# A decoder step on one core: where the index-key page copies, the bias scratch write and the input loads stand in their queues

## What is computed

```python
def swiglu(h, w_gate, w_up, w_down):
    return (jax.nn.silu(h @ w_gate) * (h @ w_up)) @ w_down

for i in range(DEPTH):                       # DEPTH = 2, D_FF = 2688
    xp = xp + 0.5 * swiglu(rmsnorm(xp, ffn_norm[i, 0]), ...)
    xs = xs + 0.5 * swiglu(rmsnorm(xs, ffn_norm[i, 0]), ...)
    # i = 0, mixer A: an indexer scores all keys, top-k of them are attended
    ki_all = concatenate([cache_idx[layer, page_table].reshape(b, past, IDX_DIM), ki], axis=1)
    # i = 1, mixer B: sliding window with sinks
    # both add rel_bias(dist, table), 32 log buckets x 16 heads
    xp = xp + 0.5 * swiglu(rmsnorm(xp, ffn_norm[i, 1]), ...)
y = rmsnorm(x, final_norm)
```

## Time and profile before

| what | us |
|---|---|
| median of 3 runs | 2751.65 (2748.27 to 2754.09) |
| span of the profiled execution, first to last instruction | 2739.2 |
| median of the runs less that span | 12.45 |
| TensorE matmuls busy | 2444.2 (89% of the span) |
| GpSimd busy | 1040.7 (38%) |
| VectorE busy | 1134.8 (41%) |
| DMA | 195.6 MB, mean 71 GB/s |

### The profile page before, as it was taken

How to read it: one execution, slowest core, us unless ns; L and a number is a source line. 1 busy time by engine, 2 the same in 40 slices (tenths; PEclk the granted TensorE clock), 3 DMA queues, 4 the chain that set the end, 5 groups by cost and what they waited for, 6 DMA issues and landing times.

```text
span 2739.2 us, 42110 instructions
## 1 busy us (share of the span) xinstructions
PE 2444.2 (89%) x16399; PEld 2236.9 (82%) x16399; DVE 1134.8 (41%) x1299; ACT 370.8 (14%) x778; POOL 1040.7 (38%) x620
## 2 busy tenths in 40 slices
PE   4999998999467676889999999999988888999997
PEld 3999998539345444889999999999986678999997
DVE  3444322147999322454443244442214435444312
ACT  2000000220123211010000010000012321000001
POOL 2556554204000000245555545555541004555552
PEclk9999999759567777999999999999996569999998
DMA  7433433503001223123333333333351002333331
GB/s 137 95 90 89 106 84 76 102 0 95 0 1 31 62 76 101 39 62 84 84 82 82 89 77 77 83 81 81 83 129 39 1 8 63 83 84 81 80 80 55
DMA packets 377742, 195.60 MB, mean 71 GB/s; under 512 B 66323, under 2 KB 374380, under 8 KB 377644
## 3 DMA queue, kind: packets, MB, share of 16 engines
q1 hardware_dynamic: 365216, 178.61, 26.4%
q10 hardware_dynamic: 12220, 15.73, 2.4%
q0 software_dynamic: 224, 0.16, 0.0%
HBM read 188.17 MB, written 11.62 MB: 73 GB/s over the span
## 4 chain that ended last, share of the span: by engine, by line
PE 81%; DVE 11%; SPq 4%; issue 2%; ACT 1%; DMA 1%; POOL 0%; DVEq 0%; ACTq 0%; POOLq 0%
PE psum L472 69%; PE psum L589 2%; DVE scsA L1445 1%; DVE mx8A L1443 1%; SPq L350 1%; SPq L385 1%; PE psum L564 1%; PE psum L659 1%; SPq L357 1%; PE psum L757 1%; PE psum L748 1%; DVE scpA L1445 1%; PE psum L579 1%; DVE mx8pA L1443 1%; PE psum L626 1%
## 5 line engine op out<-in xcount | busy, mean ns | idle before, releaser
L472 PE MATMUL psum<-XH,WSP 128*128 128x288 f32 (+1 forms) x6688 | 1171.9, 297 | 28.2 <-POOL WSP L434 13.0
L472 PEld LDWEIGHTS psum<-XH,WSP 128*128 128x128 f32 (+1 forms) x6688 | 991.5, 190 | 33.7 <-issue 13.8
L432 POOL CAST WSP<-WST 128x1024 fp32r<-128x1024 f32 (+1 forms) x305 | 310.0, 1016 | 1619.2 <-PE psum L472 1477.1
L434 POOL TENSOR_TENSOR WSP<-WST,WSP 128x1024 fp32r<-128x1024 f32 (+1 forms) x305 | 730.0, 2394 | 24.4
L472 PE MATMUL psum<-XL,WSP 128*128 128x288 f32 x3344 | 719.5, 297 | 0.0
L472 PEld LDWEIGHTS psum<-XL,WSP 128*128 128x128 f32 x3344 | 542.6, 190 | 0.0
L472 PE MATMUL psum<-GH,WSP 128*128 128x288 f32 x2688 | 465.7, 295 | 0.0
L472 PEld LDWEIGHTS psum<-GH,WSP 128*128 128x128 f32 x2688 | 394.1, 188 | 0.0
L472 PE MATMUL psum<-GL,WSP 128*128 128x288 f32 x1344 | 286.7, 295 | 0.0
L1177 DVE TENSOR_TENSOR us<-psum,rstd 128x576 f32<-128x576 f32 x84 | 63.7, 758 | 478.4 <-PE psum L472 478.4
L1150 DVE SCALAR_TENSOR_TENSOR X<-psum,X 128x576 f32<-128x576 f32 x48 | 36.4, 758 | 438.9 <-PE psum L472 438.9
(11 more groups left out here) (213 smaller groups left out, 1678.3 us busy)
## 6 DMA issues: line engine op xcount, KB each, us to landing
WST<-in_ffn_w_gate SPq DMA_DIRECT2D x168, 256.0 KB, 3.8
WST<-in_ffn_w_up SPq DMA_DIRECT2D x168, 256.0 KB, 3.9
WST<-in_ffn_w_down SPq DMA_DIRECT2D x192, 224.0 KB, 3.6
WST<-in_a_w_in SPq DMA_DIRECT2D x28, 256.0 KB, 4.6
kv0A<-in_cache_kv SPq DMA_DIRECT2D x48, 128.0 KB, 2.3
kv1A<-in_cache_kv SPq DMA_DIRECT2D x48, 128.0 KB, 2.3
WST<-in_b_w_in SPq DMA_DIRECT2D x20, 256.0 KB, 3.8
kscr<-in_cache_idx SPq DMA_DIRECT2D x128, 32.0 KB, 2.0
```

What stands on the lines that cost most here:

```text
L432: nc.gpsimd.tensor_copy(WSP[s][:, 0, 0:width], WST[s][:, 0:width]).then_inc(w_hi, 1)
L434: nc.gpsimd.tensor_tensor(WSP[s][:, 1, 0:width], WST[s][:, 0:width], WSP[s][:, 0, 0:width].bitcast(F32), ALU.subtract).then_inc(w_split, 1)
L472: ins = mm(out[0:width, h, :], w[:, part, b * width:(b + 1) * width], x[:, h * HALF:(h + 1) * HALF], start=first and k == 0, stop=last and ...
```

## The change

Three edits.

- In ffn0's gate loop the sync engine issues the six weight loads of a pass first, then the page copies of request i. The copies of request 7 stay behind the loop.
- ScalarE issues the identity, then x, then the other five constants.
- The DMA that writes gscr moves from ahead of update(0) to behind ffn0's gate loop on ScalarE, ahead of update(1), and the wait for it to behind update(1). gvec gets space of its own beside GH and GL.

```diff
@@ memory @@
             us = sb(c, "us", [P, TOK])
+            gvec = sb(c, "gvec", [HEADS, GW])
...
-            gvec = sb(c, "gvec", [HEADS, GW])
@@ sync engine, ffn @@
                 with sp.Fori(0, NF // RING) as i:
+                    for j in range(2 * RING):
+                        chunk(n0 + j, i, 2 * RING, cols((wg, wu)[j % 2], (i * RING + j // 2) * P))
                     if name == "ffn0":
                         gather_keys(i)
-                    for j in range(2 * RING):
-                        chunk(n0 + j, i, 2 * RING, cols((wg, wu)[j % 2], (i * RING + j // 2) * P))
                 if name == "ffn0":
                     for b in range(NF // RING, NB):
                         gather_keys(b)
@@ ScalarE @@
+            act.dma_start(ident[:, :], io["c_ident"]).then_inc(const_in, 16)
+            for t in range(NTT):
+                src = ...
+                act.dma_start(xtok[0:src.shape[0], t, :], src).then_inc(x_in, 16)
-            for dst, src in ((ident[:, :], io["c_ident"]), (grows[0:4 * ND, :], ...
+            for dst, src in ((grows[0:4 * ND, :], ...
                 act.dma_start(dst, src).then_inc(const_in, 16)
-            for t in range(NTT):
-                src = ...
-                act.dma_start(xtok[0:src.shape[0], t, :], src).then_inc(x_in, 16)
...
+            act.wait_ge(gain_set, 1)
+            update(0)
+            ffn("ffn0")
             act.wait_ge(g_set, 1)
             act.dma_start(bass.AP(tensor=gscr, ...), gvec...).then_inc(g_out, 16)
-            act.wait_ge(gain_set, 1)
-            update(0)
+            update(1)
             act.wait_ge(g_out, 16)
-            ffn("ffn0")
-            update(1)
```

More of the change, by code:

```diff
@@ L1000, in window_sample_attention @@
                        bank[(7, 3)[half]][0:NT, :], ACT.Copy).then_inc(ms["ptnS_evac"], 1)
-            for dst, src in ((ident[:, :], io["c_ident"]), (grows[0:4 * ND, :], io["ffn_norm"].rearrange(
+            act.dma_start(ident[:, :], io["c_ident"]).then_inc(const_in, 16)
+            for t in range(NTT):
+                src = io["x_prompt"][0, t * P:(t + 1) * P, :] if t < NQT else \
+                    io["x_sample"].rearrange("b t d -> (b t) d")
+                act.dma_start(xtok[0:src.shape[0], t, :], src).then_inc(x_in, 16)
+            for dst, src in ((grows[0:4 * ND, :], io["ffn_norm"].rearrange(
                     "l s (d p) -> (l s d) p", p=P)), (grows[4 * ND:6 * ND, :], io["mix_norm"].rearrange(
@@ L1006, in _ @@
                 act.dma_start(dst, src).then_inc(const_in, 16)
-            for t in range(NTT):
-                src = io["x_prompt"][0, t * P:(t + 1) * P, :] if t < NQT else \
-                    io["x_sample"].rearrange("b t d -> (b t) d")
-                act.dma_start(xtok[0:src.shape[0], t, :], src).then_inc(x_in, 16)
             act.wait_ge(gain_ps, 1)
```

## The result

The changed kernel runs in 2780.05 us (median of 4 runs, 2768.36 to 2784.07), the kernel before in 2750.28 (4 runs beside them): a ratio of 1.0097, 95% interval 1.0075 to 1.012. The forecast was 2781.7 (2759 to 2791), slower. The profiled execution has a span of 2778.3 us. Of all runs in this document two were slow ones, 3125.86 and 3873.18 us, both of the kernel with the write moved alone; they are in its median and not in its ratio.

A forecast was written before the change was run, and what follows sets the result against it. The prediction took TensorE, holding 81% of the chain, to bound the kernel. Start -10.6, stall +38.8 and restart +1.8 sum to +30.0 us, added to the median 2751.65: 2781.7 us, range 2759 to 2791.

The forecast's parts named there:

- step 1: Start of ffn0, loads before gathers and x moved forward: first projection at 43.7 instead of 54.27, gain 10.6 us.
- Between the passes: Gate loop of ffn0: one batch still stands between two groups of six loads, so nothing changes.
- step 2: End of the gate loop: two batches instead of one before the first down load, a stall of 16.8 us from order alone.
- step 3: End of the gate loop: batch 7's gathers meet the scratch write, making the whole stall 38.8 us (16.8 to 42.4).
- The reckoning beside the row: Batch 7 beside the write: packet turns of 2.1 to 4.0 us, the batch ending near 357 even at 2.1.
- Rival B: End of the gate loop: gathers pass at 0.79 us, the first down load meets the write; +8 to +19 us, chance 0.17.
- step 4: TensorE after the new stall: matmuls run slowly until the clock recovers, costing 1.8 us.
- The frame: Whole kernel: the median is 12.4 us over the profiled span, and the change is added to the median.

The follow-up runs named there:

- x alone: The changed kernel with the sync engine waiting for x before its first weight load: 2780.79 us, ratio 1.0112.
- The doubling: The changed kernel with a second scratch write of the same size behind the first, to a scratch nobody reads: 2812.77 us, ratio 1.0219.
- the four with pieces: Changed kernel with batch 7 in the first pass and the write cut into 8 DMAs: 2741.48 us; three variants with further start edits: 2740.57, 2756.58, 2737.37.

## Why the prediction was right

The mechanism and the place hold. The size holds in part by luck: the terms found sum to +34.2 us and those forecast to +30.0. The start was put 3.1 too good and the stall 1.4 too low, which add up, and only 0.3 of the restart goes the other way. That the medians are 29.8 apart, so close to 30.0, owes something to the matmuls' pace and to mixer A, of which the forecast had nothing.

**The start, step 1: right in kind, 3.1 us too high.** The gain was put at 10.6 (range 5.6 to 15.1) and is 7.5. The mis-sized term is the landing of x and the constants beside three weight loads: 12.7 was reckoned from the two rates, and the constants' matmul begins at 15.60. Two errors stand in that term. The reckoning took 3 x 256 KB for the three chunks, while a chunk is two DMAs of 256 KB; the list of DMA issues of the changed kernel's first 16 us has six:

```profile
WST<-in_ffn_w_gate SPq DMA_DIRECT2D x4, 256.0 KB, 11.0
...
WST<-in_ffn_w_up SPq DMA_DIRECT2D x2, 256.0 KB, 12.8
```

And it put the first byte (2 us behind the issue, which it took from no row) and the rest some 2 us too early: without its 3.0 for the loads it has 9.7, and the run with x alone has 11.91. The loads cost 3.7 us there, more than the 3.0 of half their bytes and less than the 6.0 of all of them, for the last two of the six land at 18.1 and 18.9, behind the constants. That the constants move into the path was right: their products stand right ahead of the transposes. That moving x forward gains nothing fits, too, the run with the old order (transposes at 17.34 against 17.27), but that run had a fourth load beside x and so doesn't settle it. The overlap of splits and norm was put at 1.5 us; from the transposes to the statistics' end it was 47.40 - 17.27 = 30.1 instead of 27.8, so 2.3: the splits did not end near 16 to 18 us but ran from 14.98 to 25.9, and met the first three of VectorE's longer operations (1.75, 1.58 and 1.35 us). Together 2.9 + 0.8, less 0.6 by which the first projection is recorded ahead of the statistics' end, make the 3.1. How far the two costs trade was not seen: x alone wins 3.7 and loses 3.4.

**Between the passes.** As forecast, nothing to speak of: beside the 40.2 us TensorE has one wait for a split in ffn0, of 0.6 us.

**The order at the end, step 2.** The stall from the order alone was put at 16.8; with the write early it is 15.1.

**The write, step 3.** Forecast: two quick issues, six at 4.31, chunk 42 at 356.1 in the old times, a stall of 38.8. Found: one quick, six of about 4 and one of 1.4, and 40.2. The write was put at 30.0 us and landed after 32.3. The reckoning beside the row, from the packets, has an error of its own: with turns of 2.1 us its steps end at 350.5 (two quick, twelve at 2.1, two quick), not near 357, so the sum would have been 5 us lower and not the same. And 4.31 us is the interval of the issues; a gather beside the write took 18.4 us to land. The doubling and the early write show both causes apart (65.2, 40.2, 15.1). Rival B has lost: gathers beside the write are held. But what it named as the second line is real: with the batch out of the way, the loads themselves are held and stall TensorE for 9.8 and 12.0 us. The forecast did not need that, since batch 7 had waited out the write; it had called the size of it open.

**The restart, step 4.** 1.8 forecast, 1.5 found. The windows now have clock records for it: the granted clock falls to 0.50 in the gap (second row), from the level of 2.4 GHz to that of 1.2 GHz, and the window that holds the restart has a mean of 0.63. The columns are those of rows 4.

```profile
310.00:315.00 5.00, 3.96 (x30) 3.72 (x28) 0.88 (x2) 0.00 (x0) 0.00 (x0) 1.00 0.90 102
...
320.00:325.00 5.00, 0.00 (x0) 0.00 (x0) 0.00 (x0) 0.00 (x0) 0.00 (x0) 0.50 0.90 102
...
350.00:360.00 10.00, 5.82 (x33) 5.83 (x34) 0.00 (x0) 0.00 (x0) 8.72 (x6) 0.63 0.69 154
```

**The frame.** That the median lies 12.4 us above the profiled span was used without asking why. In every execution whose time and span are both known the difference is 2.2 us, within 0.1 (2780.46 and 2778.3 for the changed kernel, 2751.27 and 2749.1 for the kernel before); the profiled execution of the kernel before was therefore some 10 us quicker than the median, and its quick pace in ffn1 is worth 9.4 of them. The sum was made of terms and added to the median, and so did not suffer by it; against the span of the profiled execution, 2769.2 was forecast and 2778.3 found.

## What to carry to other kernels

A DMA queue that carries both urgent loads and slow copies has a place for a copy only where the loads have slack: count the copies between any two loads, at the ends of a loop as well as within it, since turning "copy, load" to "load, copy" changes nothing in the loop and doubles the copies at its end. A large write is not out of the way because it stands on another engine's queue: here whatever was issued beside it waited, a load of many short runs longest, and cutting it into pieces that the ring could cover made it free. Work that is made early competes too, for the DMA engines and for VectorE: here what helped was to fill the idle stretch with the copies and to keep loads and splits out of the way of x and the norm.

## What the runs showed of the hardware

Matmuls run at two paces with the granted clock at 1.00 in both: 130.0 and 133.3 ns for the 288 columns. An execution changes from one to the other at some point and stays for hundreds of us: the kernel before had the quick one in ffn1, the changed kernel in its first 1400 matmuls or so, the one with the write back in its old place in ffn1, the one with the constants first in ffn2, the one with batch 7 in the first pass and the write early in ffn2; of the four with pieces two had a short stretch of it and two, the fastest among them, none. A feed-forward at one or the other differs by 9.4 us, more than the effect of several edits here; the times of one kernel spread accordingly (the kernel before from 2738.14 to 2758.32 beside the various experiments), which is why stages are compared above and not spans alone. What sets the pace isn't settled; no run here varied it.

A 3 MB write from 16 partitions in runs of 1.5 KB goes at some 100 GB/s, with the DMA engines 90% busy (the window from 320 to 325 us, above). It slows a half load issued beside it from 3.75 to as much as 28.24 us and a gather from 2.0 to 18.4, and the engine that issues them is held as well: after one or two quick issues, one gather goes out every 4.3 us.
